# Gated product of the feed-forward stage: kept in its PSUM bank instead of an SBUF buffer

## What is computed

```
h = _rmsnorm(x, g_pre_ffn[l]) * (1 + sc2) + sh2
f = (jax.nn.silu(h @ w_gate[l]) * (h @ w_up[l])) @ w_down[l]
x = x + ga2 * _rmsnorm(f, g_post_ffn[l])
```

## Time and profile before

| engine | busy us | share of the span | instructions |
|---|---|---|---|
| PE (matmul) | 3386.0 | 89% | 19532 |
| PEld (weight load, beside PE) | 3033.0 | 80% | 19532 |
| DVE | 1797.6 | 47% | 2807 |
| ACT | 1038.8 | 27% | 2298 |
| POOL | 1426.3 | 37% | 804 |

### The profile page before, as it was taken

One profiled execution on the slowest core, in us unless ns is written; L12 is line 12 of the kernel. 1 busy time (PEld: TensorE's weight loads), 2 busy tenths in 40 slices (PEclk: granted clock), 3 DMA queues, 4 the chain that ended last, 5 costly groups with the idle time before them and its releaser, 6 DMA issues. The chain is left out here.

```text
span 3804.7 us, 48831 instructions
## 1 busy us (share of the span) xinstructions
PE 3386.0 (89%) x19532; PEld 3033.0 (80%) x19532; DVE 1797.6 (47%) x2807; ACT 1038.8 (27%) x2298; POOL 1426.3 (37%) x804
## 2 busy tenths in 40 slices
PE   5998888888999998999988978888899999899997
PEld 2987677767888888888878777776788888888886
DVE  3116777754444534534433156786443453453333
ACT  2323555553100001200014234776320110120001
POOL 2210687810654544444530302000054454455441
PEclk7998899989999999999999988998999999999998
DMA  6205444422322223322222134112232222242222
GB/s 202 71 15 160 143 146 147 150 78 88 101 74 77 72 73 89 99 69 72 73 60 100 55 123 119 29 34 67 76 117 72 67 74 77 72 131 75 72 67 67
DMA packets 397728, 337.90 MB, mean 89 GB/s; under 512 B 107192, under 2 KB 325000, under 8 KB 397504
## 3 DMA queue, kind: packets, MB, share of 16 engines
q1 hardware_dynamic: 249808, 233.18, 20.1%
q10 hardware_dynamic: 147696, 101.61, 9.2%
HBM read 282.87 MB, written 51.87 MB: 88 GB/s over the span
## 5 line engine op out<-in xcount | busy, mean ns | idle before, releaser
L581 POOL TENSOR_SCALAR w_hi<-raw 128x1024 fp32r<-128x1024 f32 (+2 forms) x400 | 458.7, 1147 | 2270.2 <-PE ps L598 2135.0
L583 POOL TENSOR_TENSOR w_lo<-raw,w_hi 128x1024 fp32r<-128x1024 f32 (+2 forms) x400 | 975.4, 2438 | 33.4
L596 PE MATMUL ps<-w_lo,ht_hi 128*128 128x512 f32 (+2 forms) x2040 | 798.5, 391 | 145.8 <-DVE tokm L1685 83.3
L596 PE MATMUL ps<-ht_lo,w_hi 128*128 128x320 f32 x2816 | 873.3, 310 | 4.9 <-DVE ht_lo L1359 3.0
L597 PE MATMUL ps<-ht_hi,w_lo 128*128 128x320 f32 x2816 | 871.6, 310 | 0.0
L598 PE MATMUL ps<-ht_hi,w_hi 128*128 128x320 f32 x2816 | 871.5, 309 | 0.0
L597 PE MATMUL ps<-w_hi,ht_lo 128*128 128x512 f32 (+2 forms) x2040 | 787.1, 386 | 0.0
L598 PE MATMUL ps<-w_hi,ht_hi 128*128 128x512 f32 (+2 forms) x2040 | 784.9, 385 | 0.0
L596 PEld LDWEIGHTS ps<-w_lo,ht_hi 128*128 128x128 f32 x2040 | 397.8, 195 | 232.5 <-DVE tokm L1685 99.0
L596 PEld LDWEIGHTS ps<-ht_lo,w_hi 128*128 128x128 f32 x2816 | 530.0, 188 | 8.1 <-DVE ht_lo L1359 3.8
L597 PEld LDWEIGHTS ps<-ht_hi,w_lo 128*128 128x128 f32 x2816 | 530.0, 188 | 1.6
(11 more groups left out here) (127 smaller groups left out, 3681.2 us busy)
## 6 DMA issues: line engine op xcount, KB each, us to landing
raw<-in_w_gate_dram SPq DMA_DIRECT2D x88, 512.0 KB, 3.8
raw<-in_w_up_dram SPq DMA_DIRECT2D x88, 512.0 KB, 3.8
raw<-in_w_down_dram SPq DMA_DIRECT2D x88, 512.0 KB, 3.5
raw<-in_w_mod_dram SPq DMA_DIRECT2D x80, 512.0 KB, 4.3
x_rows<-tokm ACTq DMA_DIRECT2D x30, 512.0 KB, 5.0
x_old<-x_rows ACTq DMA_DIRECT2D x30, 512.0 KB, 4.3
kv_rows<-stage ACTq DMA_DIRECT2D x20, 512.0 KB, 3.3
tokm<-kv_rows ACTq DMA_DIRECT2D x30, 320.0 KB, 4.1
```

What stands on the lines that cost most here:

```text
L581: pool.tensor_scalar(hi, r, 1.0, 0.0, ALU.mult, ALU.add).then_inc(s_whi, 1)
L583: pool.tensor_tensor(lo, r, hi.bitcast(F32), ALU.subtract).then_inc(s_w, 1)
L596: pe.matmul(out, lhs[0], rhs[1], start=first, stop=False)
```

## The change

The product is written back over the bank that the up product came from, and both its readers take it from there. The buffer `gated32` and the wait for it go; `o_low` gets a small buffer of its own. Since the banks are now read until the low halves are made, the up product of the next tile waits for `s_al` instead of `s_a32`.

```diff
-        gated32 = sb("gated32", [P, 2, 320])
+        o_low = sb("o_low", [P, 2, VD])
...
-        o_low = gated32[:, :, 0:VD]
...
-                        for i, (name, done, read) in enumerate((("w_gate", s_g, s_sil), ("w_up", s_u, s_a32))):
+                        for i, (name, done, read) in enumerate((("w_gate", s_g, s_sil), ("w_up", s_u, s_al))):
...
-                        act.activation(act_ring(half, j % 4)[0][:, c * 320:(c + 1) * 320], gated32[:, c, :], ACT.Copy).then_inc(s_ah, 1)
+                        act.activation(act_ring(half, j % 4)[0][:, c * 320:(c + 1) * 320], ps[:, 2 + c, 0:320], ACT.Copy).then_inc(s_ah, 1)
...
-                        if n >= 2:
-                            dve.wait_ge(s_al, n - 1)
-                        dve.tensor_tensor(gated32[:, c, :], ps[:, 2 + c, 0:320], stage[:, c * 320:(c + 1) * 320], ALU.mult).then_inc(s_a32, 1)
+                        up = ps[:, 2 + c, 0:320]
+                        dve.tensor_tensor(up, up, stage[:, c * 320:(c + 1) * 320], ALU.mult).then_inc(s_a32, 1)
...
-                        dve.tensor_tensor(lo, gated32[:, c, :], hi.bitcast(F32), ALU.subtract).then_inc(s_al, 1)
+                        dve.tensor_tensor(lo, ps[:, 2 + c, 0:320], hi.bitcast(F32), ALU.subtract).then_inc(s_al, 1)
```

## The result

The changed kernel takes 3696.91 us (median of 4 runs, 3695.34 to 3700.85) against 3808.52 us (4 runs): a ratio of 0.9703, 95% interval 0.9691 to 0.9715. The forecast was 3693, range 3679 to 3724. One run of a later experiment, the kernel with each low half made twice, took 11391 us, three times as long as the other runs of that kernel, for a reason that was not found, and is left out.

A forecast was written before the change was run, and what follows sets the result against it. PE bounds the kernel, busy 89%, so gains come from its gaps. 93.3 + 12.4 + 10.5 = 116.2 us off the 3804.7 span gives 3688.5, plus 3.9 to the median: 3693 us; own range 3680 to 3706, 8-in-10 range 3679 to 3724.

The forecast's parts named there:

- Low half from PSUM: DVE's low half (line 1675) taking one input from the PSUM bank: 0.49 us, bounds 0.47 to 2.70.
- Product into PSUM: DVE's gated product written back over its PSUM bank: 0.49 us taken, bounds 0.47 to 1.68.
- rival 1: In-place product dear but bearable: at 1.68 us part of the stalls returns, kernel 3729 us; chance 0.08.
- High half: ACT's high-half copy reading PSUM instead of SBUF: 0.03 us less, at nothing where the first low half covers it.
- Rival 2: Low half not shortened, its median staying above 1.1 us: kernel 3808.6 us, 3806 to 3811; chance 0.04.
- rival 3: In-place product, ahead of the first addition, costs more than it frees: at 4 us, kernel 3852 us; chance 0.02.
- The moved wait: PE's next up product waiting on `s_al`: costed at nothing, with 5.5 us to spare.
- Ordinary pairs: 36 tile pairs where PE stalls in `down` for the first addition: stall goes altogether, 93.3 us gained.
- The slack of 0.4 us: In ordinary pairs, the first addition would end about 0.4 us before PE is due to issue `down`'s piece 2.
- Ends of halves: Four feed-forward half ends where PE waits for both low halves: three gain, 12.4 us together.
- The three pairs: Layer 0's second half, stalls of 6.1 to 6.4 us: 2.6 of stall plus 0.9 of half clock each, 10.5 us.
- Rival 4: The three pairs gain all of their 27 us, residual's additions slipping in ahead of POOL: 3676 us; chance 0.04.

## Why the prediction was right, step by step

- *Low half from PSUM, 0.49 us*: 486 ns. *Product into PSUM, 0.49*: 500 ns, so rival 1 falls. Its upper bound of 1.68 was no price of writing PSUM: line 1474 reads two SBUF operands, and the two of its 22 instances with 128 columns that took 665 and 671 ns are the two that ran beside POOL; the others took 286 to 301. The 668 ns given as line 1548's median are its minimum at 512 columns (the median is 681 in the earlier trace rows), which moves the estimate for 320 columns by less than 0.01 us. *High half*: 0.035 less. Rival 2 falls by the spread of the low half, rival 3 by the in-place product.
- *The moved wait at nothing*: shown by itself, ratio 1.0002.
- *Ordinary pairs, 93.3 us*: with 27.7 us everywhere the second products give back 92.2 us by the trace of before, the difference being mostly one pair that had stalled 1.29 and not 2.05 us. The slack of 0.4 us is the one that doubling the low halves showed.
- *Ends of halves, 12.4 us*: 4.1 at the one above (11.46 - 7.32), and by the same reading 4.2 and 4.7 at the two ends in layer 0 (11.50 to 7.30 and 12.02 to 7.32 us), 13.0 together.
- *The three pairs, 10.5 us*: the term that was mis-sized. The stall of the earlier trace rows is now 3.93 us, 2.2 less where I took 2.6, and so are the other two (4.20 and 3.93). The half clock after this one nearly stayed:

```profile
1500.26 0.79 PE L595 MATMUL ps<-w_lo,ht_hi 128*128 128x512 f32 x1 [3.93 <-DVE tokm L1686]
```

```profile
1500.30:1503.80 3.50, 3.50 (x8) 2.76 (x9) 1.08 (x2) 1.41 (x2) 0.85 (x1) 0.50 0.42 120
```

  (busy us of PE, PEld, DVE, ACT, POOL, then the granted clock: 0.50.) After the other two it got shorter; the 7 us behind the second stall, before and after:

```profile
1574.70:1581.70 7.00, 7.00 (x19) 5.53 (x20) 1.88 (x4) 0.00 (x0) 0.00 (x0) 0.60 0.27 77
```

```profile
1548.90:1555.90 7.00, 7.00 (x24) 5.58 (x25) 2.60 (x4) 1.44 (x2) 0.89 (x1) 0.76 0.28 79
```

  In the second products of tiles 2 to 3, 4 to 5 and 6 to 7 the change gave 2.4, 3.2 and 3.4, so 9.0 us: 2.2 each from the stall, and 0.8 on average from the half clock, where I took 0.9. The step that missed is "the low halves of the tile before, ahead of the residual, give some 0.5 to 1". Counted from tile 1's second product the residual did come 0.4 us earlier (5.8 instead of 6.2 us), but the norm behind it ends 0.55 us after POOL's `w_lo` in both kernels: at 1518.96 and at 1497.80 (1495.70 + 2.10, shown above).

```profile
1516.04 2.37 POOL L583 TENSOR_TENSOR w_lo<-raw,w_hi 128x1024 fp32r<-128x1024 f32 x1
```

```profile
1494.88 2.37 POOL L582 TENSOR_TENSOR w_lo<-raw,w_hi 128x1024 fp32r<-128x1024 f32 x1
```

  So the norm took 2.10 us where it had taken 1.80, and most of the 0.4 was lost again. Rival 4 did not happen, though much of it can be had: by the second products of this half (452.2 us from the first to the last in the changed kernel, 435.7 and 433.6 in the others) POOL's later start takes 16.5 us there and the later norm 18.6.
- *Sum, 116.2 us*: 92.2 + 13.0 + 9.0 = 114.2 by the terms, and 113.4 measured from the first to the last low half. The medians differ by 111.6. The 3.9 us between span and median were not all "what lies around it": the profiled run of the change spans 3699.0 and was timed at 3700.85, 1.9 us more. The rest is scatter between runs. So it is partly chance that the forecast missed the median by only 3.9 us: from the profiled span it missed by 10.5 (3699.0 against 3688.5), 7.5 of them ahead of the feed-forward part.

The rule on DVE's overhead from the Trainium skill (Perfetto Trace Analysis, section Optimizing Scalar/DVE Operations) would, as an estimate from its 60 and 125 ns, have made the low half 0.065 us dearer from PSUM. The runs don't agree: 486 ns from PSUM, 491 from SBUF with POOL kept away.

What does agree is the Trainium skill's SBUF — State Buffer, section Who interferes with whom: a DVE instruction with two SBUF inputs contends with a GpSimd instruction that reads SBUF, and one with at most one such input doesn't, as long as it is outside DVE's two-port performance modes. By that rule either remedy, another place for one input or another time for POOL, should do, and both did. The exception matters as well: the norm, with one tensor input, took 0.75 us with POOL idle and 2.10 beside it. In which mode it ran no row shows.

## What to carry to other kernels

Look for an instruction whose duration spreads over 481 to 2703 ns at one shape, and ask what runs beside it, whether it ends with it, and who waits behind it. Here the spread went when one operand moved to PSUM, and also, but for two instances, when the other engine started about 1.5 us later; letting the urgent work pass it in its queue left it long but, except at the ends of the loops, harmless. Price a removed stall by the distance between starts with and without it (2.37 us, not the 2.05 of idle time), count the half clock after it, and compute the slack: it tells what may still be added for nothing. Check such a price by stretches of the trace and not by the median alone: of the 32 us that the doubled low halves cost, the medians showed 24.

## What was not expected

The stage ahead of the feed-forward part scatters by 18 us between single profiled runs (first low half at 974.9 to 993.4 us), more than several of the effects that were sought, so parts were compared from a mark behind it. And three stalls of 3.9 to 4.2 us, one behind the other, were cut to 0.3 to 0.5 us by a change on an engine, POOL, that the profile does not name as what ended them.
